# Position-bias units moved: selectors and rows in another place, five units in the last downward projection, five behind the context values

## What is computed

```python
# first block, layer 1
h = rmsnorm(x, norm_ffn_pre[layer])
y = conv_ffn(h, ffn_w_up[layer], ffn_conv_w[layer], ffn_conv_b[layer], ffn_w_down[layer])
x = x + rmsnorm(y, norm_ffn_post[layer])
...
# second block, layer 0
h = modulate(rmsnorm_2(x, norm_g[l, 0]), sh1, s1)
hc = modulate(rmsnorm_2(ctx, norm_g[l, 0]), csh1, cs1)
kc, vc = jnp.split(hc @ w_in[:, cuts[1]:], 2, axis=-1)
z, q, k, v = jnp.split(h @ w_in, cuts, axis=-1)
...
# position bias in neighborhood_attention
dr = row_idx - rows[:, None] + WIN_H - 1
dc = jnp.clip(cols[None, :] - cols[:, None] + WIN_W - 1, 0, 2 * WIN_W - 2)
bias = rpb[:, dr[:, None, :, None], dc[None, :, None, :]].astype(jnp.float32)
```

## Time and profile before

| | |
|---|---|
| median of 3 runs | 2548.91 us (2548.86 to 2550.6) |
| the profiled execution | 2550.53 us |
| its span in the trace | 2548.7 us |
| PE busy | 2485.8 us, 98% |
| DVE busy | 1535.5 us, 60% |
| ACT busy | 1071.2 us, 42% |
| POOL busy | 90.4 us, 4% |
| mean granted clock of PE | 0.992 of full |

### The profile page before, as it was taken

One profiled execution on the slowest core, in us unless ns is written; L12 is line 12 of the kernel. 1 busy time (PEld: TensorE's weight loads), 2 busy tenths in 40 slices (PEclk: granted clock), 3 DMA queues, 4 the chain that ended last, 5 costly groups with the idle time before them and its releaser, 6 DMA issues.

```text
span 2548.7 us, 32885 instructions
## 1 busy us (share of the span) xinstructions
PE 2485.8 (98%) x13141; PEld 2008.9 (79%) x13141; DVE 1535.5 (60%) x2571; ACT 1071.2 (42%) x1761; POOL 90.4 (4%) x126
## 2 busy tenths in 40 slices
PE   8999999999999989999999998999999999999999
PEld 7887788888876667888878876888888776888887
DVE  7455776877456646746566255666653897534433
ACT  4444543334435655433345345423223654422323
POOL 2000001000000000000000000011100000000000
PEclk9999999999999999999999999999999999999999
DMA  6323335554221122332324221366653331233331
GB/s 180 113 83 100 91 108 173 157 165 140 61 90 55 54 75 73 101 100 90 92 84 153 83 66 42 111 203 192 193 153 91 92 101 58 91 93 98 99 96 53
DMA packets 286159, 271.16 MB, mean 106 GB/s; under 512 B 11811, under 2 KB 270167, under 8 KB 286007
## 3 DMA queue, kind: packets, MB, share of 16 engines
q1 hardware_dynamic: 267143, 210.33, 27.1%
q0 software_dynamic: 15088, 54.40, 7.2%
q10 hardware_dynamic: 3776, 4.34, 0.6%
HBM read 262.72 MB, written 2.10 MB: 104 GB/s over the span
## 4 chain that ended last, share of the span: by engine, by line
PE 92%; DVE 4%; ACT 2%; issue 1%; DMA 1%; SPq 0%; ACTq 0%; DVEq 0%
PE G L2598 71%; PE G L2614 7%; PE G L2553 4%; PE M L2151 1%; PE M L919 1%; PE M L1301 1%; PE M L929 1%; PE M L1312 1%; PE M L1290 1%; DVE SQ L2365 1%; PE M L1766 1%; PE M L1777 1%; DVE w_lo L596 1%; PE M L2646 0%; DMA sel<-const_sel 0%
## 5 line engine op out<-in xcount | busy, mean ns | idle before, releaser
L596 DVE TENSOR_TENSOR w_lo<-raw,w_hi 128x1024 fp32r<-128x1024 f32 x396 | 482.6, 1224 | 625.0 <-ACT w_hi L591 623.7
L2598 PE MATMUL G<-H_hi,w_hi 128*128 128x512 f32 (+1 forms) x1952 | 771.4, 395 | 5.8 <-DVE H_lo L407 2.4
L2598 PE MATMUL G<-H_hi,w_lo 128*128 128x512 f32 (+1 forms) x1952 | 758.6, 389 | 0.0
L2598 PE MATMUL G<-H_lo,w_hi 128*128 128x512 f32 (+1 forms) x1952 | 758.3, 388 | 0.0
L591 ACT ACTIVATE w_hi<-raw 128x1024 fp32r<-128x1024 f32 x396 | 416.4, 1055 | 811.1 <-PE G L2598 703.5
L2598 PEld LDWEIGHTS G<-H_hi,w_hi 128*128 128x128 f32 x1952 | 368.1, 189 | 102.3 <-issue 27.1
L2598 PEld LDWEIGHTS G<-H_hi,w_lo 128*128 128x128 f32 x1952 | 367.4, 188 | 76.7
L2598 PEld LDWEIGHTS G<-H_lo,w_hi 128*128 128x128 f32 x1952 | 368.0, 189 | 72.6 <-issue 0.8
L2598 PE MATMUL G<-hid_hi,w_hi 128*128 128x512 f32 x752 | 293.1, 390 | 2.7 <-DVE Y L747 2.7
L2598 PE MATMUL G<-hid_hi,w_lo 128*128 128x512 f32 x752 | 292.6, 389 | 0.0
L2598 PE MATMUL G<-hid_lo,w_hi 128*128 128x512 f32 x752 | 292.5, 389 | 0.0
(11 more groups left out here) (409 smaller groups left out, 2703.1 us busy)
## 6 DMA issues: line engine op xcount, KB each, us to landing
raw<-in_w_ff SPq DMA_DIRECT2D x128, 512.0 KB
mod_w<-in_w_mod POOLq DMA_DIRECT2D x96, 512.0 KB, 4.5
raw<-in_ffn_w_up SPq DMA_DIRECT2D x176, 256.0 KB
raw<-in_ffn_w_down SPq DMA_DIRECT2D x32, 512.0 KB
raw<-in_w_in SPq DMA_DIRECT2D x28, 512.0 KB
raw<-in_mlstm_w_in SPq DMA_DIRECT2D x24, 512.0 KB
raw<-in_kv_w SPq DMA_DIRECT2D x16, 512.0 KB
raw<-in_fox_w_qg SPq DMA_DIRECT2D x16, 512.0 KB
```

The costliest lines, as they stand in the source:

```text
L596: dve.tensor_tensor(w_lo[:, j, :], raw[:, j, :], w_hi[:, j, :], ALU.subtract).then_inc(lo_done, 1)
L2598: mm = pe.matmul(G[:, 2 * p + m, 0:n], lw[:, k, ms], rh[:, t, 0:n], start=(t == 0 and q == 0), stop=(t == st["ktiles"] - 1 and q == 2), sk ...
```

## The change

Three tiles move to other addresses: `sel` from 112 K to 164 K, `rp` from 136 K to 172 K, `rm` from 137 K to 172.5 K. POOL no longer waits for the end of `f1_down2` before it fills and loads `rp` and issues the first two selector loads. They come directly behind the load of the context tokens. PE transposes the rows ahead of `f1_up2`, with a new wait for all eight copies `ct_c` (the transpose writes a bank that they read). ACT copies the rows out behind the fifth group of `f1_up2`. Units 0 to 4 go into `f1_down2`: on PE between `first_two` and group 2, on ACT behind the first two splits. Units 5 to 9 stay behind `c_v`, their evacuations between the tiles of the fill.

```diff
--- before.py
+++ after.py
@@ -251,11 +251,11 @@
         bn_parts = at("bn_parts", 175 * K, [P, 16, 6])
         nL = [[at(f"nL{e}_{b}", where, [P, T]) for b, where in enumerate(places)]
               for e, places in enumerate(((188 * K, 190 * K, 192 * K, 194 * K), (196 * K, 198 * K, 200 * K, 173 * K)))]
-        sel = at("sel", 112 * K, [P, 2, 16 * HP])
+        sel = at("sel", 164 * K, [P, 2, 16 * HP])
         even_sq = at("even_sq", 120 * K, [P, 2, T])
         even_sum = at("even_sum", 124 * K, [P, T])
-        rp = at("rp", 136 * K, [120, P])
-        rm = at("rm", 137 * K, [P, 2, 8, 8])
+        rp = at("rp", 172 * K, [120, P])
+        rm = at("rm", 172 * K + 512, [P, 2, 8, 8])
         yp = at("yp", 112 * K, [P, 2, T + 2 * PAD])
         yp_turned = [at(f"yp_turned{d}", 117 * K + 4608 * (d - 1), [P, 2, T + 2 * PAD]) for d in range(1, COPIES)]
         conf_squared = at("conf_squared", 144 * K, [P, DT, T])
@@ -671,6 +671,8 @@
                             act.wait_ge(ct_c, t + 1)
                             act.wait_ge(n_ss, 8 * NORM["ctx"] + t - 1)
                             act.activation(ct_sq[:, t % 2, :], ct[:, t, :], ACT.Square).then_inc(n_sq, 1)
+                    if layer == 1 and part == 2 and g == 4:
+                        bias_rows_act(act)
 
                 steps = group_steps(act, f"f{layer}_up{part}", split_hi, up)
                 if part == 0:
@@ -689,8 +691,14 @@
                 def down(i, p, g):
                     act.activation(two(Y, g), G[:, 2 * p:2 * p + 2, :], ACT.Copy).then_inc(pair_read[p], 1)
 
-                groups(act, f"f{layer}_down{part}", split_hi,
-                       (down, None, squares_act(act, f"fpost{layer}", Y, f"f{layer}_down2"))[part])
+                steps = group_steps(act, f"f{layer}_down{part}", split_hi,
+                                    (down, None, squares_act(act, f"fpost{layer}", Y, f"f{layer}_down2"))[part])
+                if layer == 1 and part == 2:
+                    next(steps)
+                    next(steps)
+                    for u in range(EARLY_UNITS):
+                        bias_act(act, u)
+                finish(steps)
 
         def ffn1_dve(dve, link, layer, spare=None):
             base = HIDDEN[f"f{layer}"]
@@ -811,7 +819,6 @@
             mod_loads(pool, 0, 48)
             pool.wait_ge(fx["y"], FOX_HEADS // 2)
             pool.dma_start(ctx_tm[:], a["ctx_2"].rearrange("a (b p) d -> p (a b) d", p=P)).then_inc(ctx_dma, 16)
-            pool.wait_ge(chunk_used, used_after("f1_down2"))
             pool.memset(rp[:], NEG).then_inc(setup_p, 1)
             pool.wait_ge(setup_p, 3)
             for c in range(0, P, 32):
@@ -1628,8 +1635,11 @@
                 sp.dma_start(out_v[:, :, part], x_tm[:, :, part]).then_inc(done, 16)
             sp.wait_ge(done, 64)
 
+        EARLY_UNITS = 5
+
         def bias_rows_pe(pe):
             pe.wait_ge(rp_dma, 64)
+            pe.wait_ge(ct_c, 8)
             pe.transpose(M[:, 2, 0:120], rp[:], ident[0:120, 0:120]).then_inc(tb_t, 1)
 
         def bias_bank(u):
@@ -2088,18 +2098,14 @@
                 next(keys)
             squares_behind("fpost1")(3, 1)
             finish(keys)
-            bias_rows_pe(pe)
             vals = linear_units("c_v", H_hi, H_lo, "T", need=from_h("ctx"), n=CTX)
             for _ in range(3):
                 next(vals)
-            pe.wait_ge(tb_r, 8)
-            for u in range(4):
-                bias_unit(pe, u)
             pe.wait_ge(n_ss, 8 * NORM["even"] + 7)
             pe.wait_ge(n_sd, NORM["even"])
             pe.matmul(M[:, 0, :], ones[:], even_sum[:], start=True, stop=True).then_inc(n_ss, 1)
             finish(vals)
-            for u in range(4, 10):
+            for u in range(EARLY_UNITS, 10):
                 bias_unit(pe, u)
             near_pe(pe, linear, linear_units, from_h, squares_behind)
 
@@ -2193,7 +2199,6 @@
                 for t in tiles:
                     squared(t)
             finish(keys)
-            bias_rows_act(act)
             values = group_steps(act, "c_v", split_hi, values_out)
             next(values)
             squared(6)
@@ -2201,14 +2206,12 @@
             squared(7)
             next(values)
             next(values)
-            for u in range(4):
-                bias_act(act, u)
             norm_act(act, "even", None, None)
             act.wait_ge(chunk_used, used_after("c_v"))
             for t in range(DT):
                 fill_act(act, "even", None, lambda t: mods[0][:, t:t + 1], None, T, None, (t,))
-                if t < 6:
-                    bias_act(act, 4 + t)
+                if t < 10 - EARLY_UNITS:
+                    bias_act(act, EARLY_UNITS + t)
             finish(values)
             near_act(act)
             groups(act, "n_out", split_hi, squares_act(act, "mlp0", X, "n_out"))
@@ -2752,6 +2755,8 @@
 
                 for part in range(3):
                     need = from_h(f"ffn{layer}")
+                    if layer == 1 and part == 2:
+                        bias_rows_pe(pe)
                     if part == 0:
                         first_two(f"f{layer}_up0", H_hi, H_lo, need, by_tiles(DT), between)
                     linear(f"f{layer}_up{part}", H_hi, H_lo, need=need,
@@ -2760,6 +2765,10 @@
                     need = lambda t, part=part: pe.wait_ge(hid_l, base + FFN_FIRST[part] + t + 2)
                     if part:
                         first_two(f"f{layer}_down{part}", hid_hi, hid_lo, need, by_chunks(FFN_TILES[part]))
+                        if layer == 1 and part == 2:
+                            pe.wait_ge(tb_r, 8)
+                            for u in range(EARLY_UNITS):
+                                bias_unit(pe, u)
                         if behind:
                             behind(0, 0)
                     linear(f"f{layer}_down{part}", hid_hi, hid_lo, need=need, behind=behind)
```

## The result

The changed kernel takes 2565.43 us (median of 4 runs, 2564.86 to 2566.41) against 2549.61 us before, a ratio of 1.0063 with the 95% interval 1.0051 to 1.0074. It is slower by 15.8 us. The forecast was 10.3 us slower, with a range that ended at 2564.5. A second measurement on another occasion gave 2562.13 us against 2549.81, 1.0050 (1.0036 to 1.0063). The sign and the places were right, the size was too small. The profiled execution took 2564.86 us, its span 2563.1, which is 14.4 us more than before.

A forecast was written before the change was run, and what follows sets the result against it. PE, busy 98% of the span, was taken as the bound, so gains come only where it idles. Terms 4.1 + 6.6 - 3.8 + 3.4 = +10.3 us on the median 2548.91 gave 2559.2 us, range 2553 to 2564.5.

The forecast's parts named there:

- Edit 1: Transpose of the rows ahead of `f1_up2`: PE waits 3.8 us for the eighth context copy, +4.1 us.
- edit 4: Units 0 to 4 in `f1_down2`: unit 4 waits for selector load 2 and group 2 starts later, +6.6 us.
- the first two parts: Stretch to the end of `first_two`, 4.1 + 1.7 us; then units 0 to 4 through 36 `c_k` products, 6.6 + 1.7.
- edit 5: Seam: units 0 to 3 no longer ahead of the sum, load 4 still awaited, `n_u` starts earlier, -3.8 us.
- The term for the clock: Half-rate spells of PE, one behind each of the two new stalls, about 1.7 us each, +3.4 us.
- a sign of being wrong: The prediction is wrong if, among other signs, the stage from `n_u` on takes another time than before.
- rival of the spells that fall away: Old half-rate spells, costing PE up to 8.5 us, may go and no new ones come: -1.6 us, 2547.3 us; 10%.
- the clock forgives: Rival: one or none of the two new stalls is followed by a half-rate spell, 2555.8 to 2557.5 us; 20%.
- the selectors come slowly: Rival: loads 2 and 4 take 7.1 us, spells longer, +14.6 to +18.0 us; 13% with anything above 12.5 us.
- Fast loads: Rival: both selector loads take 4.0 us and no spell follows, +5.0 us, 2553.9 us; 5%.
- it would not be slower: Whole kernel: chance of faster 0.04 and of same, within 0.2%, 0.13, against slower 0.83.
- work as meant: Rival: faster by more than 5.1 us, needing a seam gain above 3.8 and both waits nil; something faster 2%.

The follow-up runs named there:

- e1: The changed kernel with the transpose of the rows moved behind the fourth group of the same upward projection; 2556.11 us, 1.0029 of the kernel before.
- e6: The changed kernel with four early units in the last downward projection in place of five, two selector buffers; 2555.19 us, 1.0022 of the kernel before.
- e4: The changed kernel with the transpose behind the fourth group and four selector buffers together; 2548.13 us, 0.9996 of the kernel before.
- e3: The changed kernel with small products that nobody reads filling PE's idle stretches in all four places; 2558.37 us, 1.0034 of the kernel before.
- e9: The changed kernel with unread products at the seam alone, ahead of the sum of squares and of unit 8; 2559.01 us, 1.0037 of the kernel before.
- e5: The changed kernel with its units back in their old places, the rest of the change kept; 2556.74 us, 1.0031 of the kernel before.

## Why the prediction was wrong in size

**Right: the two stalls.** Edit 1 was said to cost a wait of 3.8 us, and it is 3.72; edit 4 a wait of about 4 us ahead of unit 4, and it is 4.88 (the load took 6.30 us where I had taken 5.9, and went out 0.45 us behind unit 1 where I had taken 0.3). With unit 4 at half rate (1.83 us against 1.04) the term of 6.6 measured 7.9. With one spell behind each stall the first two parts came to 5.8 and 8.7 against 5.8 and 8.3. e1 and e6 take away each stall by itself, and e4 shows that without them the rest of the change costs nothing measurable in sum. That ACT, held in the evacuation of unit 4, was not the next bound also held: behind that unit the chain has PE's 120 products in one piece (1339.98 to 1364.41), with no wait for the splits of group 3.

**Wrong: edit 5, the seam, -3.8 us, which measured -0.8.** The order was as said: sum right behind the last gathering, units 5 to 7, a wait of about 2 us for load 4. The step that failed is the one on the clock. I counted spells behind the two big stalls alone, and priced the seam from rows at full rate, although I had a row with 0.51 behind an idle stretch of 2.1 us, and the edit itself made one of 1.85 us ahead of the sum and turned waits of 1.1 us into one of 2.14. At half rate the end of the values cost 1.5 us more (5.50 against 3.99) and units 8 and 9 another 1.4 (3.51 against 2.08). That is 2.9 of the 3.0 us that were missing. e3 and e9 show it as cause: with PE kept busy there, in e9 only there, the two stretches are back at 4.0 and 2.1 us. The term for the clock, 3.4 us with bounds 0 and 6.8, should have had four places and 6.4 us, as e3 measured it.

With 6.4 in place of 3.4 the sum is +13.3 us, where the profiles differ by 14.4 and the medians by 15.8 and, in the second measurement, by 12.3. That second median, 2562.13, lies inside the range, so how far off the number was depends in part on the occasion. The two missing spells do not: both measurements have a stage of 179 us.

**Not foreseen: +1.4 us from `n_u` on,** which the prediction itself had named as a sign of being wrong. One more half-rate window stands at 2144.3, some 740 us behind the last edited instruction. At the same place before (2131.2) the rate was full. From `n_u` to the end the profiles of this study lie between 1155.9 and 1160.2 us with the same work. A spell of 10.2 us near 1533 is as long in the change, and it is missing in the profile of e1, whose part from `n_u` on is 3.9 us shorter. My rival of the spells that fall away had this mechanism and the wrong sign for this change. What decides where they fall was not tested. The change's two profiled executions are 2.7 us apart with stages within 0.2 us: 1.3 us lie ahead of the last context transposes and 1.7 from `n_u` on. That the two medians, 3.3 us apart, differ for the same reason is argued; no run shows it.

**The rivals.** That the clock forgives is out (0.60 and 0.56 behind the two stalls). That the selectors come slowly held in small part: load 2 took 6.30 us where 7.1 were supposed, load 4 4.05. The number of that rival, 2563.5 to 2566.9 us, takes in the measured 2565.43, but by luck: it had the seam's gain cut by a slow load 4, and it was cut by the clock. Fast loads are out. That it would not be slower is out. The change does not work as meant, because both things that it moved forward were bound to something that had not moved: the transpose to DVE's copies, and the fifth unit to a load that waits for the units in front of it.

## What to carry to other kernels

Before a piece of work is moved into a busy engine's list, look up for each of its inputs when it is there, and put the piece behind that point, in an idle stretch that exists already: spread over such gaps the ten units left the kernel 6.8 us faster than before, and in the places of the change it was 12 to 16 us slower. A loop of loads that waits for its own consumers moves with them, so a unit that is one too many brings a whole load time with it. And when a stall is priced on TensorE, every idle stretch of about two microseconds or more in the new order is priced with the half-rate spell that may follow it, those that the change makes by removing work too.

## What the runs showed of the hardware

- Idle stretches of 1.85 to 4.9 us of PE were followed by windows of about 3.4 us near half rate in all four new places of the change. Filling them with products that nobody reads returned 6.4 us of 179.0 without removing any wait. The gap of 2.7 us in the downward projection had none behind it before and had one in e5, so one execution does not tell whether a gap of that length brings a spell.
- Nor does every short gap bring one. In e6 PE waits 1.95 us ahead of the sum of squares, and in e1 2.18 us ahead of the third chunk of the values. The granted clock behind both is 1.00, where behind the change's 1.85 and 2.18 us in the same places it is 0.55 and 0.57. The gap and the window, e6 first:

```profile
1380.93 1.12 PE L2106 MATMUL M<-even_sum,ones 128*128 128x512 f32 x2 [1.95 <-DVE even_sum L814]
1381.00:1384.40 3.40, 3.40 (x24) 2.92 (x24) 2.15 (x2) 1.33 (x2) 0.00 (x0) 1.00 0.67 189
...
1375.58 0.35 PE L2617 MATMUL G<-w_hi,H_hi 128*128 128x256 f32 x1 [2.18 <-DVE w_lo L596]
1375.60:1379.00 3.40, 3.08 (x24) 2.88 (x24) 3.40 (x6) 1.90 (x3) 0.00 (x0) 1.00 0.48 157
```

- The Trainium skill (TensorE: Matmul & The Clock Gate, "HAM oscillation — how this bites in real kernels") tells of idle gaps for loads that let the clock fall, each anew. The change's trace agrees behind its two waits for a selector load, 4.88 us (0.56) and 2.14 us (0.50).
- A load of 512 KB issued by GpSimd took 4.0 to 7.1 us from issue to landing before and 4.05 and 6.30 us in the change's chain.
